# Tiles transposed by VectorE block transposes with a store and a load, and inputs given in the layout that is needed

## What is computed

```python
def hybrid_layer(x, ...):
    p = rms_norm(x, norm_g) @ w_in
    qk, v, o, z_a, ig, fg, xb, z_b = jnp.split(p, SPLIT_AT, axis=-1)
    qk = jax.nn.silu(causal_dwconv(qk, qk_conv))
    ...
    h = mlstm_chunkwise(q, k, v, i_pre, log_f)
    ...
    y_a = h.astype(x.dtype) * jax.nn.silu(z_a)
    xc = causal_dwconv(xb, lru_conv_w) + lru_conv_b
    y_b = rg_lru(xc, w_a, b_a, w_x, b_x, lam) * jax.nn.silu(z_b)
    return x + jnp.concatenate([y_a, y_b], axis=-1) @ w_out

def second_block(x, mem, ...):
    mem_n = rms_norm_2(mem, mem_norm_g)
    for i in range(DEPTH_2):
        h = rms_norm_2(x, norm_g[i])
        z = h @ w_in
        mix_out = gmlp_spatial_gating(...)  # or forgetting_attention, differential_attention
        mem_out = memory_attention(mq, mk, mv)
        branch = jnp.concatenate([mix_out, mem_out], axis=-1) * jax.nn.silu(gate)
        x = x + branch @ w_out[i]
```

## Time and profile before

| | us |
|---|---|
| median of 3 runs | 3273.44 |
| lowest, highest | 3273.06, 3273.78 |
| span of the profiled execution | 3271.3 |
| PE busy in it | 3257.1 (100%) |
| DVE busy | 2082.9 (64%) |
| ACT busy | 1830.6 (56%) |
| POOL busy | 174.0 (5%) |

### The profile page before, as it was taken

One profiled execution on the slowest core, in us unless ns is written; L12 is line 12 of the kernel. 1 busy time (PEld: TensorE's weight loads), 2 busy tenths in 40 slices (PEclk: granted clock), 3 DMA queues, 4 the chain that ended last, 5 costly groups with the idle time before them and its releaser, 6 DMA issues.

```text
span 3271.3 us, 39485 instructions
## 1 busy us (share of the span) xinstructions
PE 3257.1 (100%) x15142; PEld 2708.7 (83%) x15142; DVE 2082.9 (64%) x2843; ACT 1830.6 (56%) x2394; POOL 174.0 (5%) x241
## 2 busy tenths in 40 slices
PE   9999999999999999999999999999999999999999
PEld 7888888888888888888888888888888888888887
DVE  6558655756757755657667565665555667757664
ACT  5555545546665455546665565555556555565553
POOL 2000000000000000000000000000000321200000
PEclk9999999999999999999999999999999999999999
DMA  8666666565566666565567666556656565575565
GB/s 274 211 205 196 200 194 187 191 192 176 181 208 197 192 195 197 183 201 174 186 211 228 189 206 193 183 176 190 193 185 207 173 183 181 191 228 188 180 198 174
DMA packets 395740, 637.77 MB, mean 195 GB/s; under 512 B 102108, under 2 KB 104484, under 8 KB 395168
## 3 DMA queue, kind: packets, MB, share of 16 engines
q1 hardware_dynamic: 382928, 601.50, 59.2%
q0 software_dynamic: 10336, 27.45, 2.7%
q10 hardware_dynamic: 2288, 6.30, 0.5%
HBM read 608.10 MB, written 6.62 MB: 188 GB/s over the span
## 4 chain that ended last, share of the span: by engine, by line
PE 94%; ACT 2%; DVE 2%; DMA 1%; issue 1%; SPq 0%; ACTq 0%
PE acc L1727 29%; PE acc L1729 29%; PE acc L1728 29%; DVE weights_lo L1272 1%; PE tr L1814 1%; ACT weights_hi L946 1%; PE nm L1917 1%; ACT work L1012 1%; PE tr L1796 0%; PE tr L1727 0%; ACT work L1005 0%; PE tr L1729 0%; PE tr L1905 0%; PE tr L1728 0%; SPq L768 0%
## 5 line engine op out<-in xcount | busy, mean ns | idle before, releaser
L1272 DVE TENSOR_TENSOR weights_lo<-weights_raw,weights_hi 128x1024 fp32r<-128x1024 f32 x1103 | 1340.6, 1229 | 953.3 <-ACT weights_hi L946 950.0
L946 ACT ACTIVATE weights_hi<-weights_raw 128x1024 fp32r<-128x1024 f32 x1103 | 1156.0, 1057 | 1003.4 <-PE acc L1729 919.1
L1727 PE MATMUL acc<-weights_hi,u_hi 128*128 128x512 f32 x3136 | 1237.5, 395 | 0.0
L1729 PE MATMUL acc<-weights_hi,u_lo 128*128 128x512 f32 x3136 | 1222.6, 390 | 0.0
L1728 PE MATMUL acc<-weights_lo,u_hi 128*128 128x512 f32 x3136 | 1221.4, 389 | 0.0
L1727 PEld LDWEIGHTS acc<-weights_hi,u_hi 128*128 128x128 f32 x3136 | 588.9, 188 | 124.7 <-issue 4.0
L1729 PEld LDWEIGHTS acc<-weights_hi,u_lo 128*128 128x128 f32 x3136 | 588.5, 188 | 123.6
L1728 PEld LDWEIGHTS acc<-weights_lo,u_hi 128*128 128x128 f32 x3136 | 589.0, 188 | 119.3
L1727 PE MATMUL acc<-weights_hi,y_hi 128*128 128x512 f32 x1280 | 501.6, 392 | 0.9 <-DVE y_lo L1276 0.3
L1729 PE MATMUL acc<-weights_hi,y_lo 128*128 128x512 f32 x1280 | 498.6, 390 | 0.0
L1728 PE MATMUL acc<-weights_lo,y_hi 128*128 128x512 f32 x1280 | 498.2, 389 | 0.0
(11 more groups left out here) (285 smaller groups left out, 1957.7 us busy)
## 6 DMA issues: line engine op xcount, KB each, us to landing
weights_raw<-in_w_in_dram SPq DMA_DIRECT2D x384, 512.0 KB, 3.9
weights_raw<-in_w_out_dram SPq DMA_DIRECT2D x256, 512.0 KB, 4.4
weights_raw<-in_a_w_in_dram SPq DMA_DIRECT2D x176, 512.0 KB, 4.2
weights_raw<-in_b_w_in_dram SPq DMA_DIRECT2D x112, 512.0 KB, 3.7
weights_raw<-in_c_w_in_dram SPq DMA_DIRECT2D x112, 512.0 KB, 4.3
weights_raw<-in_w_mem_kv_dram SPq DMA_DIRECT2D x63, 512.0 KB, 5.1
kv_scratch<-work ACTq DMA_DIRECT2D x8, 512.0 KB, 5.3
qk_tiles<-in_w_a_dram POOLq DMA_DIRECT2D x8, 512.0 KB, 4.4
```

What stands on the lines that cost most here:

```text
L946: SC_E.activation(WH[:, b % RING], RAW[:, b % RING], ACT.Copy).then_inc(sem("hi_done"), 1)
L1272: V.tensor_tensor(WL[:, b % RING], RAW[:, b % RING], WH[:, b % RING].bitcast(F32), ALU.subtract).then_inc(sem("lo_done"), 1)
L1727: T.matmul(dst, hi_l, hi_r, start=start, stop=False, **kw)
L1729: return T.matmul(dst, lo_l, hi_r, start=False, stop=stop, **kw)
```

## The change

Of the 57 PE tiles 40, and all 39 crossbar tiles, go a third way. A piece `flip` turns each 32x32 block of a 128x1024 pair on DVE with one instruction, POOL stores the flipped pair with four DMAs to a scratch in DRAM, and a piece `fetch` eleven slots later in SP's queue loads it back with the blocks in their transposed places. The user stands eight slots behind the flip: `join` (ACT writes the high half directly) with `low` one slot on, `cjoin`, `qt` or `lrz`. There are 75 flips in ten buffers that share five scratch lanes; a flip waits for its lane's last fetch. The memory's tokens, the residual's x3, each layer's last mixer group, the memory query of the two gMLP layers and the last group's keys stay on PE.

Because the results come later, pieces move: `lru_in(p + 1)` now runs ahead of `lru_gate(p)`, attention of the first two groups begins four or five slots later, the last convolution of q/k moves into the gate rows, and the first w_out product is a pair of chunks.

The x tokens, the spatial weights and biases and the parameter columns are given to the kernel a second time in the layout that it needs, so `mgain`, the transposes of `params` and those of `wst` are gone, and new pieces `in` split x's transposed tokens on ACT and DVE. The identity and the first tokens are loaded from ACT's queue, and the first block's matmuls begin with the high half.

```diff
-ISSUE, JOIN, LOW = 7, 5, 2
+FETCH, JOIN, LOW = 11, 8, 1
+LANE = {"u0": "uq", "q": "uq", "a0": "uq", "u1": "um", "m": "um", "x": "xz", "z": "xz", "n": "n",
+        "a": "ab", "b": "ab"}
+LANES = ("uq", "um", "xz", "n", "ab")
...
-    def apart(slot, src, ready, buf):
-        q = pl.piece(slot, "apart", src=src, ready=ready, buf=buf)
-        pl.piece(slot + ISSUE, "turn", at=q, buf=buf)
+    def turn(slot, src, ready, buf):
+        q = pl.piece(slot, "flip", src=src, ready=ready, buf=buf)
+        pl.piece(slot + FETCH, "fetch", at=q, buf=buf)
         return q
-    def xbar(slot, src, ready, dst, kt0, gain, buf, join=JOIN):
-        q = apart(slot, src, ready, buf)
-        p = pl.piece(slot + join, "join", dst=dst, kt0=kt0, gain=gain, at=q, buf=buf)
-        pl.piece(slot + join + LOW, "low", at=p, buf=buf)
+    def bounce(slot, src, ready, dst, kt0, gain, buf):
+        q = turn(slot, src, ready, buf)
+        p = pl.piece(slot + JOIN, "join", dst=dst, kt0=kt0, gain=gain, at=q, buf=buf)
+        pl.piece(slot + JOIN + LOW, "low", at=p, buf=buf)
         return p
+    def keys_in(hn, **kw):
+        q = turn(pl.here() + 1, "n", ("hn_out", hn), "n")
+        q.twin = pl.piece(pl.here() + 8, "qt", at=q, buf="n", **kw)
...
-                q = apart(pl.here() + 1, "xt", ("cq_x", cq), "q")
-                pl.piece(pl.here() + 5, "cjoin", at=q, buf="q")
-                for r in range(2):
-                    pl.piece(pl.here() + 7 + r, "conv", to="cq", r=r, l=l, taps=QC + 4 * j, at=q)
-                pl.piece(pl.here() + 9, "cqs", j=j)
+            q = turn(pl.here(), "xt", ("cq_x", cq), "q")
+            pl.piece(pl.here() + 8, "cjoin", at=q, buf="q")
+            for r in range(2):
+                pl.piece(pl.here() + 9 + r, "conv", to="cq", r=r, l=l, taps=QC + 4 * j)
+            pl.piece(pl.here() + 11, "cqs", j=j)
...
-            ya.append(tp(s + 8, "o", ("mf_out", mf), "y", 12, gain) if p == 3 else
-                      xbar(s + 8, "o", ("mf_out", mf), "y", 4 * p, gain, "m"))
+            ya.append(bounce(s + 6, "o", ("mf_out", mf), "y", 4 * p, gain, "m"))
...
-            pl.piece(pl.here() + 1, "ct", to="cx", at=cx)
+            q = turn(pl.here(), "xt", ("cx_x", cx), "x")
+            pl.piece(pl.here() + 8, "cjoin", at=q, buf="x")
             for r in range(2):
-                pl.piece(pl.here() + 2 + r, "conv", to="cx", r=r, l=l, taps=LW + 4 * p, bias=LB + 4 * p)
-            c = pl.here() + 1
-            c += 4 if p == 0 else 2
+                pl.piece(pl.here() + 9 + r, "conv", to="cx", r=r, l=l, taps=LW + 4 * p, bias=LB + 4 * p)
+            c = pl.here() + 10
+            if p:
+                pl.piece(pl.here(), "load_wax", l=l, p=p)
             for w in range(2):
-                pl.piece(pl.here() + 4 + w if p == 0 else pl.here() - 2 + 2 * w, "wax", w=w)
+                pl.piece(pl.here() + 4 + 2 * w, "wax", w=w)
             pl.piece(c + 1, "cvs")
             for w in range(2):
                 pl.piece(c + 3 + w, "lgate", l=l, p=p, w=w)
+            c += 2 * (p > 0)
             pl.piece(c + 5, "lru", l=l, p=p)
             pl.piece(c + 6, "lrq", l=l, p=p)
             pl.piece(c + 6, "lri", l=l, p=p)
...
         def lru_gate(p):
             zb = pl.chunk(("w_in", l, COL_ZB + CH * p, 0), "tok", "u", "zb")
-            pl.piece(pl.here() + 3, "cz", at=zb)
-            pl.piece(pl.here() + 5, "lrz", l=l, p=p)
-            lr.append(pl.piece(pl.here() + 7, "lry", l=l, p=p))
+            q = turn(pl.here(), "xt", ("zb_out", zb), "z")
+            pl.piece(pl.here() + 8, "lrz", l=l, p=p, at=q)
+            lr.append(pl.piece(pl.here() + 10, "lry", l=l, p=p))
         pl.piece(pl.here() + 5, "load_wax", l=l, p=0)
         lru_in(0)
-        for j in range(4):
-            pl.chunk(("w_out", l, CH * j, 0), "tok", "y", "ox", j=j, store=False,
-                     need=tiles(ya) if j == 0 else None)
+        pl.pair(*((("w_out", l, CH * j, 0), "tok", "y", "ox", dict(j=j, store=False)) for j in range(2)),
+                (6, 8), need=tiles(ya))
+        for j in range(2, 4):
+            pl.chunk(("w_out", l, CH * j, 0), "tok", "y", "ox", j=j, store=False)
         for p in range(4):
-            if p:
-                pl.piece(pl.here(), "load_wax", l=l, p=p)
-                lru_in(p)
+            if p < 3:
+                lru_in(p + 1)
...
-                          xbar(o + 1, "x%d" % j, ("ox_out", ox), "u", 4 * j, gain, "u%d" % (j % 2)))
+                          bounce(o, "x%d" % j, ("ox_out", ox), "u", 4 * j, gain, "u%d" % (j % 2)))
...
-                ts.append(attention(kind, grp, h - 3 if kind == "B" else h - 4))
+                ts.append(attention(kind, grp, h + 1 if grp < 2 else h - 3 if kind == "B" else h - 4))
...
-                    if p.kind == "turn":
-                        wait(sp, "half_in", p.at)
-                        sp.dma_start_transpose(turned(p.buf), halves(p.buf)).then_inc(sem("half_t_" + p.buf), 16)
+                    if p.kind == "fetch":
+                        if p.buf in ("q", "x"):
+                            wait(sp, "cj_out", p.at.last.get("cjoin"))
+                        elif p.buf == "z":
+                            wait(sp, "lrz_y", p.at.last.get("lrz"))
+                        elif p.buf == "n":
+                            wait(sp, "qt_out", p.at.last.get("qt"))
+                        else:
+                            wait(sp, "jn_lo", p.at.last.get(("low", p.buf)))
+                        sp.wait_ge(sem("spilled_" + LANE[p.buf]), 64 * (p.nth + 1))
+                        sp.dma_start(turned(p.buf), SPILL[LANE[p.buf]].rearrange("b r a e -> (b r) (a e)")
+                                     ).then_inc(sem("fetched_" + LANE[p.buf]), 16)
...
+                    if k == "flip":
+                        wait(pool, "flipped", p)
+                        for a in range(4):
+                            pool.dma_start(SPILL[LANE[p.buf]][:, :, a].rearrange("b r e -> r b e"),
+                                           flipped(p.buf)[32 * a:32 * a + 32].rearrange("p (b e) -> p b e", b=4)
+                                           ).then_inc(sem("spilled_" + LANE[p.buf]), 16)
...
                     elif k == "join":
-                        act.wait_ge(sem("half_t_" + p.buf), 16 * (p.at.nth + 1))
-                        for t in range(2):
-                            to = joined(p.buf)[:, :, P * t:P * t + P].bitcast(U16).rearrange("p f (k s) -> p s f k", s=2)
-                            i = SC_E.activation(to, turned(p.buf)[:, 8 * t:8 * t + 8].rearrange("p (s f) k -> p s f k", s=2),
-                                                ACT.Copy)
-                        i.then_inc(sem("half_out"), 1)
-                        wait(act, "half_out", p)
+                        act.wait_ge(sem("fetched_" + LANE[p.buf]), 16 * (p.at.nth + 1))
                         wait(act, "mm_done", p.used.get(p.dst))
-                        hi, x = ACTS[p.dst][0], joined(p.buf)
-                        for h in range(2):
-                            j, k_ = 2 * h, p.kt0 + 2 * h
+                        hi = ACTS[p.dst][0]
+                        for j in range(4):
+                            dst = quarters(hi[:, p.kt0 + j])
                             if p.gain is None:
-                                i = SC_E.activation(hi[:, k_:k_ + 2], x[:, j:j + 2], ACT.Copy)
-                            elif p.gain[2] == 0:
-                                i = SC_E.activation(hi[:, k_:k_ + 2], x[:, j:j + 2], ACT.Copy, scale=param(p.gain, 0))
+                                i = SC_E.activation(dst, by_feature(p.buf, j), ACT.Copy)
                             else:
-                                for e in range(2):
-                                    i = SC_E.activation(hi[:, k_ + e], x[:, j + e], ACT.Copy, scale=param(p.gain, j + e))
-                            i.then_inc(sem("jn_hi"), 1)
+                                i = SC_E.activation(dst, by_feature(p.buf, j), ACT.Copy, scale=param(p.gain, j))
+                            if j % 2:
+                                i.then_inc(sem("jn_hi"), 1)
...
+                    elif k == "flip":
+                        ref(dve, p.ready)
+                        if p.nth:
+                            dve.wait_ge(sem("fetched_" + LANE[p.buf]), 16 * p.nth)
+                        if p.buf == "q":
+                            wait(dve, "mo_out", last.get("mo"))
+                            dve.wait_ge(sem("kv_st"), 16 * 8)
+                            dve.wait_ge(sem("tb_st"), 16)
+                        src = {"xt": XT, "o": O, "n": NBUF}.get(p.src)
+                        if src is None:
+                            src = X[:, :, CH * int(p.src[1]):CH * int(p.src[1]) + CH]
+                        V.transpose(flipped(p.buf).rearrange("p (b q s) -> p q b s", b=4, q=8), src
+                                    ).then_inc(sem("flipped"), 1)
...
-                        for j in range(2):
```

(6 more changed lines are left out.)

400 lines of the change are left out of this document (189 added, 211 removed), and 1 row of the table BANKS.

## The result

The changed kernel takes 3301.74 us (median of four runs, 3299.9 to 3302.89) against 3273.58 us for the kernel before: a ratio of 1.0083 with an interval of 1.0071 to 1.0095. It is 28 us slower, beyond the top of the range, 3298. The profiled execution has a span of 3301.1 us (before: 3271.3).

What follows compares the result with a forecast made beforehand. PE was taken as the bound, busy 3257.1 of 3271.3 us. Gains of 45.8 us and new waits of 42.8 us gave a span of 3268.3, so 3270 us; range 3225 to 3298, own case 3255 to 3285.

Steps and rivals of the forecast that it cites:

- PE's gains: Transposes taken off PE, 37.9 us, and old waits gone, 5.5 and 1.4 us; with 1 us at the start, 45.8 us.
- New waits: PE waits for operands queued behind DVE's added work in recurrence, gate rows and differential attention: 42.8 us in all.
- the windows' splits: Recurrence, two windows in each of two layers: weight splits on DVE come 1.2, 0.5 and 0.8 us late.
- the gate products: Recurrence windows: the convolved part's low half, which these products need, ends 2.0 us after PE wants it.
- the last part: Last part of the recurrence, twice: the output product waits 5.4 us for y's low half, 10.8 us in all.
- gate rows: Last convolution between the gates' serial steps: splits 2.8 and 0.6 us late, twice, 6.8 us in all.
- Differential attention: Head norm and final scaling fall in one slot on DVE: PE waits 3.6 us, twice, 7.2 us.
- elsewhere ... the same count leaves 0.7 us or more: mLSTM windows, part 0 and 1, gMLP, forgetting attention, layer ends: at least 0.7 us of room, so no new wait.
- The start: Identity and first tokens by ACT's queue, first block starting on its high half: a gain of about 1 us, an estimate.
- The bursts are absorbed: Rival: ACT and DVE overlap better than the serial count, so only PE's gains are left, 3228 us; chance 0.22.
- The flip costs twice: Rival: a flip takes 2.45 us on DVE, adding 17 to 20 us, 3288 us; chance 0.14.
- The spill lands late: Rival: spills landing past 10 us delay SP's weight loads; 0.5 us over on 75 tiles gives 3307 us; chance 0.07.

Runs made afterwards that it cites:

- the last kernel: Changed kernel with z gate earlier, gate rows, memory keys (last three layers), scaling (five slots) and gate products later, start loads on SP: 3262.59 us, 0.9966 of the kernel before.
- its test: Changed kernel with each of the 75 flips done twice on DVE, the second over the first: 3334.79 us, 1.0181 of the kernel before.
- the kernel with five slots: Changed kernel with differential attention's final scaling and what follows five slots later for the first two groups: 3303.07 us, 1.0087 of the kernel before.

## Why the prediction was wrong

*PE's gains: right.* The flip at 1.24 us (1.23 taken), the 40 tiles, the waits for `x_rows` gone, the spills in time for the weight loads. The table's stretches without new waits give the tile's 0.87 back.

*New waits, in the places that were named: right within 2 us.* Gaps of PE in the trace of after, beside the forecast: the windows' splits 1.12, 0.42 and 0.53 (1.2, 0.5, 0.8); the gate products 2.0 at each of four places (2.0), with 1.6 more at one of them by the clock; the last part 5.42 twice (5.4); gate rows 3.28 and 0.47, 3.26 (2.8 and 0.6, twice). Differential attention was 4.60 (3.6); its chain is the one foreseen, with a head norm that starts 0.9 later than counted. Together 43.4 us, 42.8 forecast. Terms that lie so close owe something to chance, since each was given to 1 us.

*The step that failed* is the sentence that "elsewhere ... the same count leaves 0.7 us or more". It names other places, and the memory layers are not among them; where it does name part 0, its gate products wait 0.7 us in each layer. I counted DVE's queue at each place and took ACT to have only gained room. At the memory's keys the late piece is on ACT: a piece that the change puts eight slots behind its flip falls behind a store, 9.4 us of waits.

*The start had the wrong sign.* I took 1 us as a gain; it costs 7.0 us by the fifth block. The diff moves two loads to another queue, and I priced the wait that goes, not the landing of 5.24 us that comes. That queue explains 3.4 us of it; the later landing of a weight load, the rest, is open.

*The clock was left out.* Each long wait was priced at its own length. PE's clock fell after eight waits, 15.4 us more. Before the change the granted clock is full everywhere, so no row showed that a wait has a second price.

*The sum* then closes to some 3 us. In span: 3271.3 - 44.8 (the gains without the start) + 43.4 + 9.4 + 7.0 + 15.4, and 2.8 for a wait of 1.4 at 1773 us and 1.4 at the gate products of part 0, is 3304.5; the trace has 3301.1. The three missed terms are 31.8 us, and the forecast's span and the trace's lie 32.8 apart; they moved the kernel out of the range.

*The rivals.* "The bursts are absorbed" failed as a forecast. In the last kernel some 33 us (30 of waits, 3.2 of clock) still stand between it and 3228. "The flip costs twice" did not occur; its test showed that its price was 25 us by the span and 32 by the time. "The spill lands late" did not occur. By the page "VectorE: DVE Perf Modes" of the Trainium skill, section "The three transpose paths", a flip would have been 2.5 us, an estimate from its 311 ns for one 128x128 tile of bf16; the rows have 1.24 us for eight f32 tiles in one instruction, so the figure does not carry over. Section 3.8 of the Trainium skill's "Vector Engine (DVE) Microarchitecture Reference", one element per cycle per lane, fits: 1.24 us is what the other full passes take (1.22).

*Open:* why the weight load at 15.23 us took 9.53 us to land; whether the small waits of the last kernel can go.

## What to carry to other kernels

Moving work off the bounding engine pays only as far as the in-order engines that feed it have room at that very place: here the 44.8 us that PE was to gain came back as 43.4 us of foreseen waits before anything went wrong. Walk every queue past every moved piece, the stores that it now stands behind among them, in all layers and not in the crowded ones alone. Price a long wait of PE at more than its length where the clock may fall after it, and look for the slot to which a late piece can move before taking the change as a loss: moves by one to five slots and two loads put back made 28 us of loss into 11 us of gain, though one of the moves, the scaling's, gave nothing by itself.

## What the runs showed of the hardware

PE's granted clock fell to its lower level after seven waits of 3.26 to 6.55 us and one of 1.97 us and was back at 1.00 within some 6 us; products of 512 columns followed each other by 0.43 us in that time (0.227 else). Waits of one length fell out both ways. Of four waits of 2.0 us at gate products one lost the clock. The wait of 3.28 us at the gate rows kept it in the changed kernel, and in the kernel with five slots the same wait, 3.26 us, lost it, for 2.8 us.

Two windows of the latter kernel, after its wait of 3.6 us in attention:
```profile
2720.00:2724.00 4.00, 3.50 (x8) 2.84 (x9) 4.00 (x5) 0.00 (x0) 3.98 (x8) 0.50 0.71 142
2724.00:2728.00 4.00, 4.00 (x14) 3.17 (x13) 1.80 (x2) 1.06 (x1) 3.98 (x10) 0.73 1.04 383
```
The clock is 0.50 while PE works for 3.50 of 4 us and comes back only in the window after. The store of V from ACT's queue took 6.12 us to land. POOL issued a spill in 0.55 us (80 in 43.7) beside a DVE that is busy 66%, and the spills landed in 3.0 to 4.4 us.
